# Second mixer: ScalarE takes eleven of VectorE's sixteen copies of the backward context columns

## The chip, the cores and the metric

The program runs on one core of a Trainium2 chip. The metric is the device time of one execution in microseconds; lower is better. A core has five engines with an instruction stream each: TensorE (PE in the profile, its weight loads PEld), VectorE (DVE), ScalarE (ACT), GpSimd (POOL) and SyncE (SP, which here only issues transfers). They meet through semaphores alone. TensorE writes its results to PSUM (eight banks of 512 fp32 columns on 128 partitions); VectorE and ScalarE read them from there.

## What is computed

The reference is a two-layer backbone over 512 latent and 256 context tokens of width 1024. Layer 0 is a recurrent and attention mixer with a mixture of experts (MoE) behind it; layer 1 is a grouped state-space mixer (S5) with a gated output (GLU) and a second MoE. The change lies in the S5 mixer. Cut to what matters:

```python
# 64 groups of 16 channels, 64 complex states each; once forward, once backward
for di, rev in enumerate((False, True)):
    _, h_ctx = s5_scan(u_c, lam_bar, b_bar, c_mat, h0, rev, False)   # context: 256 tokens
    yl_d, _  = s5_scan(u,   lam_bar, b_bar, c_mat, h_ctx, rev, True) # latents: 512 tokens
    y = y + yl_d
# s5_scan: h[t] = lam_bar * h[t-1] + b_bar @ u[t];  y[t] = Re(c_mat @ h[t])
glu(y)   # gelu, a 1024 x 2048 product, val * sigmoid(gate)
```

## The kernel before

The S5 mixer is the function `s5_mixer`. Tokens are taken in chunks of eight: the 256 context tokens make 32 chunks (NCC), the 512 latent tokens 64 (NCL), together 96 (NCK). For each of the 64 groups TensorE makes the state that a chunk adds to the recurrence. The forward direction lies on partitions 0 to 63 and the backward one on 64 to 127, so that both run in one scan over chunks. Real and imaginary part are two "parts" of a group.

Four groups make a half block (hb, sixteen of them, NHB), eight groups a block (b, eight of them, NB). The steps around the change, in order:

1. **Chunk sums.** For each hb TensorE waits for its factors in R (`r_in`, 512 KB a half block from HBM, seven buffers, a buffer loaded anew when the product that read it is done) and from hb 4 on for the copies of hb-4, since PSUM holds four half blocks. It then issues the products of lines 2478 and 2480 and raises `v_mm`.
2. **Copies out of PSUM into VH.** ScalarE makes two for each hb: line 2222, the latent columns of both directions (128 partitions, 512 elements), and line 2223, the forward context columns (64 partitions, 256 elements). Each raises `va_done`. VectorE makes the third, line 2350: the backward context columns (partitions 64 to 127, 256 elements), which raises `vd_done`. It waits for ScalarE's first copy of the same hb.
3. **Pairing** (`sweep`, lines 2337 to 2345). For each block b four VectorE operations (stages 0 to 3, 128 partitions, 752 elements) combine neighbouring chunks. Stage 0 waits for all copies of the block's two half blocks. VectorE's order is written out by hand: in the loop over hb each copy is followed, from hb 2 to 13, by a stage of blocks 0 to 3 (`divmod(hb - 2, 3)`, the fourth stage behind the third); blocks 4 to 7 follow when all copies are made.
4. **The scan** (lines 2374 to 2390) on VectorE: four levels over the context chunks, then 31 steps (STEPS) of four small operations in a chain.
5. **Filling in** (`fill`, lines 2400 to 2405, then `states`, line 2409) on VectorE, block by block, ScalarE making the other half of the states (line 2228). Ahead of it stands `dve.wait_ge(S['mod_mm'], LATE)`: the states are written to a tile, XS, in which weights of the modulation product have lain.
6. Meanwhile TensorE, when **all** copies of step 2 are made (`va_done`, `vd_done`), runs a chain of its own: for each block the product with the latents inside a chunk ("T", line 2506, a Toeplitz factor loaded by eight 64 KB transfers, line 2128), and between these the late modulation products n = 0 to 7 (LATE = 8; lines 1609 and 1613), for the parts of `mod_w` that the rest of layer 1 needs. Products 0 to 4 follow T(0) to T(4), one each; 5, 6 and 7 come together before T(5).
7. `from_states` (line 2520) adds the states' part for each block, `turn` (line 2531) transposes it after the gelu, and the GLU product (line 2551) starts when all eight blocks are turned.

SP's queue gives the order of transfers. Behind the R loads and the first two Toeplitz factors it waits for `v_mm` = 16, issues three 1 MB loads (line 2136), and then goes on as here:

```python
            for n in range(3, LATE):
                sp.wait_ge(S['mod_mm'], n - 2)
                sp.dma_start(w[n % 3], mod_weights(io, *MOD_LATE[n // 2], n % 2)).then_inc(m_in[n % 3], 16)
                toeplitz(n - 1)
            toeplitz(LATE - 1)
```

Each of these loads of modulation weights is 2 MB (line 2139), and `toeplitz(b)` waits for T(b-2). Products 0 to 2 read weights that ScalarE asked for before step 2 (line 2218).

Behind `turned` VectorE runs fifty small memsets (line 2425), each waiting for the one before, and only then waits for the first GLU product. The MoE behind the mixer is a loop over blocks of up to 64 or 128 tokens of one expert, six of each kind to a trip (UNROLL); its code is placed behind the mixer's in every engine's stream.

Of the kernel before, what the change touches and what calls it, by code (L numbers as in the profile page):

```python
# [10 lines left out]
ACT = mybir.ActivationFunctionType  # L11
AX = mybir.AxisListType

P = 128
# [2006 lines left out]
def s5_mixer(nc, io, st):  # L2021

    NCL, NCC = 64, 32
# [4 lines left out]
    with nc.cleanup_on_exit(), ctx:  # L2029
# [3 lines left out]
        def sem(name):  # L2033
            return nc.alloc_semaphore(f"{name}_s")
# [7 lines left out]
        VH = UV[:, NCK * SG:].rearrange("p (n a g) -> p n a g", a=2, g=SG)  # L2042
# [35 lines left out]
        S = {n: sem(n) for n in names.split()}  # L2078
# [7 lines left out]
        NHB, NB = SG // 4, SG // GB  # L2086
# [6 lines left out]

        LATE = 2 * len(MOD_LATE)

        def v_of(hb):
            return ps[:, (hb % 4) * 1024:(hb % 4 + 1) * 1024].rearrange("p (g a e) -> p g a e", g=4, a=2)

        def pairs(b):
            g = slice(b * GB, (b + 1) * GB)  # L2100
            return VH[:, 0:NCK - 2:2, :, g], VH[:, 1:NCK - 2:2, :, g]

        def scratch(j):
            return XS[:, j * NPAIR * 2 * GB:(j + 1) * NPAIR * 2 * GB].rearrange("p (n a g) -> p n a g", a=2, g=GB)

        def factor(level, which, n, g):
            return lam[:, level, which, :, g].rearrange("p (o a) g -> p o a g", o=1).to_broadcast([P, n, 2, GB])
# [70 lines left out]
        def _(act):  # L2178
# [40 lines left out]
            for hb in range(NHB):  # L2219
                act.wait_ge(S['v_mm'], hb + 1)  # L2220
                gs = slice(4 * hb, 4 * hb + 4)
                act.activation(VH[:, NCC:NCK, :, gs].rearrange("p c a g -> p g a c"), v_of(hb)[:, :, :, NCC:NCK], ACT.Copy).then_inc(S['va_done'], 1)
                act.activation(VH[0:64, 0:NCC, :, gs].rearrange("p c a g -> p g a c"), v_of(hb)[0:64, :, :, NCK:P], ACT.Copy).then_inc(S['va_done'], 1)

            def states(b):
                g = slice(b * GB, (b + 1) * GB)
                act.wait_ge(S['fill'], 4 * (b + 1))
                act.activation(SV[0:64, :, g, :], VH[0:64, NCC - 1:NCK - 1, :, g].rearrange("p c a g -> p a g c"),
                               ACT.Copy).then_inc(S['sf_done'], 1)
# [36 lines left out]
        def _(dve):  # L2266
# [60 lines left out]
            def sweep(b, stage):  # L2327
                even, odd = pairs(b)
                g = slice(b * GB, (b + 1) * GB)
                a, c = scratch(0), scratch(1)  # L2330
                n = 4 * (b - 0)
                if stage == 0:
                    if n:
                        dve.wait_ge(S['up'], n)
                    dve.wait_ge(S['va_done'], 4 * (b + 1))
                    dve.wait_ge(S['vd_done'], 2 * (b + 1))
                    dve.tensor_tensor(a, even, factor(0, 0, NPAIR, g), ALU.mult).then_inc(S['up'], 1)
                if stage == 1:
                    dve.tensor_tensor(c, even, factor(0, 1, NPAIR, g), ALU.mult).then_inc(S['up'], 1)
                if stage == 2:  # L2340
                    dve.wait_ge(S['up'], n + 1)
                    dve.tensor_tensor(a, a, odd, ALU.add).then_inc(S['up'], 1)
                if stage == 3:
                    dve.wait_ge(S['up'], n + 3)
                    dve.tensor_tensor(odd, a, c[:, :, ::-1, :], ALU.add).then_inc(S['up'], 1)

            dve.wait_ge(S['xres_in'], 16 * 8)
            for hb in range(NHB):
                dve.wait_ge(S['va_done'], 2 * hb + 1)
                dve.tensor_copy(VH[64:P, 0:NCC, :, 4 * hb:4 * hb + 4].rearrange("p c a g -> p g a c"), v_of(hb)[64:P, :, :, 0:NCC])\  # L2350
                   .then_inc(S['vd_done'], 1)
                if 2 <= hb < 14:
                    b, third = divmod(hb - 2, 3)
                    sweep(b, third)
                    if third == 2:
                        sweep(b, 3)
            for b in range(4, NB):
                for stage in range(4):
                    sweep(b, stage)
            dve.wait_ge(S['up'], 4 * NB)  # L2360
# [3 lines left out]
            for level in range(1, 5):  # L2364
# [3 lines left out]
                a, b = t1[:, 0:n], t2[:, 0:n]  # L2368
# [12 lines left out]
            for q in range(STEPS):  # L2381
                prev, here = VH[:, NCC - 1 + 2 * q], VH[:, NCC + 1 + 2 * q]
                a, b = t1[:, q % 2], t2[:, q % 2]
# [28 lines left out]
            def turned(b):  # L2412
                dve.wait_ge(S['zT_mm'], b + 1)
                dve.tensor_copy(zT[:, b, :], ps[:, b * 512:(b + 1) * 512]).then_inc(S['zt_dve'], 1)
# [6 lines left out]
            dve.wait_ge(S['o_mm'], NW)  # L2421
            for b in range(0, NB, 2):
                turned(b)
            for _ in range(50):
                done(dve.memset(sqr[:, 0, 0, 0:1], 0.0))
                done.wait()
            dve.wait_ge(S['gb_in'], 32)
            dve.wait_ge(S['xres_in'], 16 * 8)
            for u in range(8):
                n, m = divmod(u, 4)  # L2430
                val, gat = (ps[:, (2 * (u % 4) + j) * 512:(2 * (u % 4) + j + 1) * 512] for j in range(2))
                c = slice(n * 512, (n + 1) * 512)
                a, b = sv[u % 2], sg[u % 2]
# [14 lines left out]
        def _(pe):  # L2448
# [19 lines left out]
            for hb in range(NHB):  # L2468
                pe.wait_ge(S['u_done'], 16)
                pe.wait_ge(S['u_act'], 4)  # L2470
                pe.wait_ge(r_in[hb % NR], 16 * (hb // NR + 1))
                if hb >= 4:
                    pe.wait_ge(S['va_done'], 2 * (hb - 3))
                    pe.wait_ge(S['vd_done'], hb - 3)
                for g in range(4):
                    for part in range(2):
                        at = (hb % 4) * 1024 + g * 256 + part * P
                        pe.matmul(ps[0:64, at + NCC:at + P], Rb[hb % NR][:, g, part, 0:64], U[:, hb * 4 + g, :],
                                  start=True, stop=True, skip_group_check=True)
                        last = pe.matmul(ps[64:P, at:at + NCK], Rb[hb % NR][:, g, part, 64:P], U[:, hb * 4 + g, ::-1],  # L2480
                                         start=True, stop=True, skip_group_check=True)
                last.then_inc(S['v_mm'], 1)
            pe.wait_ge(S['va_done'], 2 * NHB)
            pe.wait_ge(S['vd_done'], NHB)

            def out_of(b, h, q):
                return ps[64 * h:64 * h + 64, b * 512 + q * P:b * 512 + (q + 1) * P]
# [70 lines left out]
def program(nc, io, out):  # L2558
# [4 lines left out]
    with ExitStack() as ctx:  # L2563
        x = ctx.enter_context(nc.sbuf_tensor("x", [P, NT0, D], F32))
        cT = ctx.enter_context(nc.sbuf_tensor("cT", [P, KD, 2], F32))
        io['modrow'] = dram('modrow', (2, 2, 6 * D))
        io['s5_r'] = dram('s5_r', (P, SG // 4, 4 * 2 * P))
        io['s5_w'] = dram('s5_w', (P, SG // GB, 2 * SL * GB * SI))
        io['s5_kt'] = dram('s5_kt', (SG, 32, 15 * SI))
        io['s5_l8'] = dram('s5_l8', (P, 4 * SG))  # L2570
        moe_h, table = dram('moe_h', (NTOK, D)), dram('item_table', (P, 8), I32)
        moe_acc = [dram(f'moe_acc{k}', (NTOK, D)) for k in range(2)]
        io['primer'] = dram('primer', (4, P))

        def x_final(t):

            steps = out[0].rearrange("(c s) d -> s c d", s=SL)
            return [(slice(64 * j, 64 * j + 64), steps[2 * t + j]) for j in range(2)]

        with ExitStack() as early:  # L2580
            head = {name: early.enter_context(nc.sbuf_tensor(name, shape, F32)) for name, shape in
                    (('rows', [P, NT0, D]), ('ident', [P, P]), ('modc', [P, 2, 2, KD]))}
            prepare(nc, io, {'x': x, 'cT': cT, **head})
            mixer0(nc, io, {'x': x, **head})
        moe_blocks(nc, io, {'x': x, 'moe_h': moe_h, 'moe_acc': moe_acc, 'item_table': table},
                   0, NTOK, NT0 - NL)
        s5_mixer(nc, io, {'x': x, 'cT': cT, 'moe_acc': moe_acc})
        moe_blocks(nc, io, {'x': x, 'moe_h': moe_h[0:LAT], 'moe_acc': [a[0:LAT] for a in moe_acc], 'item_table': table,
                            'x_out': x_final}, 1, LAT, 0)
# [15 lines left out]
```

## Time and profile before

| | |
|---|---|
| median of 3 runs | 2506.55 us (2506.09 to 2510.54) |
| the profiled execution | 2506.16 us, its span 2504.4 us |
| mean granted clock of TensorE | 0.952 |
| TensorE, VectorE, ScalarE, GpSimd busy | 86%, 44%, 20%, 17% of the span |
| the stretch of the chunk sums and their copies | 1515.9 to 1548.8 us |
| pairing / scan / filling in | to 1563.4 / 1606.3 / 1638.6 us |
| GLU product | from 1645.5 us |

Times within the execution count from the start of the span. In a row "idle before" is the time that the engine stood still ahead of an instruction, with the one that ended it. A granted clock of 1.00 is 2.4 GHz, 0.50 is 1.2 GHz.

### The profile page before, as it was taken

Reading aid. Unit: us, or ns where it says so; the run is one execution under the profiler, and the core shown is the slowest. Engines: PE = TensorE matmul, PEld = TensorE weight load, DVE = VectorE, ACT = ScalarE, POOL = GpSimd, SP = SyncE. Lnnn points to the kernel's source line nnn. Section 1 sums busy time; section 2 is a strip of 40 time slices with the busy share of each in tenths; the row PEclk is TensorE's granted clock in tenths of the full one; section 3 lists DMA queues with packets and bytes.
Section 4 is the critical chain, followed back from the end, with each engine's and each line's share of the span. In section 5 each row is a group of like instructions: output and inputs, shape, how many; then the busy total and the mean of one; then the engine's idle time right before and its main releaser. Section 6 shows DMA issues by size and latency. Waiting matters only on the chain. (4 is left out here: it accounts for less than half of the span.)

```text
span 2504.4 us, 40476 instructions
## 1 busy us (share of the span) xinstructions
PE 2143.6 (86%) x11989; PEld 1189.9 (48%) x11990; DVE 1092.3 (44%) x2311; ACT 509.8 (20%) x945; POOL 433.9 (17%) x359
## 2 busy tenths in 40 slices
PE   5889999997999999999999816699789999988874
PEld 3765444744544444444444405354444444444442
DVE  8853365944543333333333338942532222222222
ACT  3443233611121111111111125220221111100000
POOL 1000000002012222222222210000122222232332
PEclk9999999998999999999999968799799999999997
DMA  9971002003799999999999669830499999899996
GB/s 358 386 265 46 34 34 84 1 1 131 264 346 355 354 358 357 359 351 350 355 358 358 202 158 329 275 146 0 160 404 375 361 363 358 274 390 372 385 385 207
DMA packets 173622, 666.72 MB, mean 266 GB/s; under 512 B 37666, under 2 KB 48898, under 8 KB 129882
## 3 DMA queue, kind: packets, MB, share of 16 engines
q1 hardware_dynamic: 121410, 564.71, 58.7%
q0 software_dynamic: 36160, 64.84, 11.0%
q10 hardware_dynamic: 15960, 35.96, 4.1%
q8 instruction: 56, 0.92, 0.1%
q14 instruction: 36, 0.29, 0.0%
HBM read 617.29 MB, written 86.09 MB: 281 GB/s over the span
## 5 line engine op out<-in xcount | busy, mean ns | idle before, releaser
L1518 PE MATMUL banks_l<-slotw_l,xTw_l 128*128 128x512 f32 x800 | 358.2, 601 | 27.7 <-issue 27.7
L1529 PE MATMUL banks_l<-slotn_l,xTn_l 128*64 128x256 f32 x2816 | 325.0, 383 | 34.5 <-issue 34.5
L1529 PEld LDWEIGHTS banks_l<-slotn_l,xTn_l 128*64 128x64 f32 x2816 | 212.0, 137 | 178.9 <-issue 104.8
L1518 PEld LDWEIGHTS banks_l<-slotw_l,xTw_l 128*128 128x128 f32 x800 | 148.5, 191 | 239.3 <-issue 239.3
L1568 PE MATMUL banks_l<-slotn_l,late_l 128*64 128x512 f32 x704 | 189.9, 615 | 19.6 <-DVE late_l L1356 17.9
L1547 PE MATMUL banks_l<-slotw_l,late_l 128*128 128x512 f32 x400 | 191.8, 602 | 15.4 <-DVE late_l L1338 15.4
L977 POOL DMA_INDIRECT xgw_l<-moe_h,idxw_l x58 | 60.6, 1045 | 741.0 <-PE banks_l L1463 367.1
L1005 POOL DMA_INDIRECT moe_acc<-late_l,idxn_l x88 | 151.2, 1718 | 190.5 <-DMA moe_acc<-late_l,idxn_l 172.5
L937 POOL IOTA slotw_l<- 128x1 f32 x2 | 0.3, 140 | 729.1 <-POOLq L69 431.3
L1335 DVE TENSOR_TENSOR late_l<-late_l,banks_l 128x256 f32<-128x256 f32 x50 | 21.0, 421 | 240.2 <-ACT late_l L1107 240.2
L556 PE MATMUL ps_a<-W_a,hT_a 128*128 128x512 f32 x288 | 124.9, 595 | 0.0
L1107 ACT ACTIVATE late_l<-banks_l 128x256 f32<-128x256 f32 x50 | 19.2, 384 | 509.6 <-PE banks_l L1518 509.6
L983 POOL DMA_INDIRECT xgn_l<-moe_h,idxn_l x96 | 103.4, 1077 | 83.5 <-DVE idxn_l L1285 56.1
L1270 DVE TENSOR_TENSOR onehotn_l<-iota_slot_l,rank_l 128x512 bf16 (+1 forms) x98 | 79.3, 809 | 86.2 <-issue 86.2
L2551 PE MATMUL ps_s<-UV_s,ZU_s 128*128 128x512 f32 x256 | 110.1, 592 | 0.7 <-ACT ZU_s L2238 0.7
L1112 ACT ACTIVATE late_l<-banks_l 128x128 f32<-128x128 f32 x88 | 24.4, 278 | 417.5 <-PE banks_l L1529 417.5
L1547 PEld LDWEIGHTS banks_l<-slotw_l,late_l 128*128 128x128 f32 x400 | 68.5, 191 | 71.3 <-issue 71.3
L994 POOL DMA_INDIRECT moe_acc<-yw_l,idxw_l x50 | 79.4, 1589 | 131.3 <-DVE yw_l L1362 131.3
L1045 ACT ACTIVATE xTw_l<-banks_l 128x512 f32<-128x512 f32 x108 | 64.5, 598 | 153.1 <-PE banks_l L1463 148.6
L1338 DVE COPY late_l<-banks_l 128x256 f32<-128x256 f32 x50 | 21.2, 425 | 160.2 <-PE banks_l L1537 160.2
L1263 DVE TENSOR_TENSOR onehotw_l<-iota_slot_l,rank_l 128x768 bf16 (+1 forms) x60 | 51.9, 865 | 84.4 <-issue 84.4
L556 PEld LDWEIGHTS ps_a<-W_a,hT_a 128*128 128x128 f32 x288 | 55.3, 192 | 68.4 <-issue 68.0
(433 smaller groups left out, 3235.0 us busy)
## 6 DMA issues: line engine op xcount, KB each, us to landing
slotn_l<-in_exp_w_gate SPq DMA_DIRECT2D x88, 1024.0 KB
slotn_l<-in_exp_w_up SPq DMA_DIRECT2D x88, 1024.0 KB
slotn_l<-in_exp_w_down SPq DMA_DIRECT2D x88, 1024.0 KB, 12.1
slotw_l<-in_exp_w_gate SPq DMA_DIRECT2D x50, 1024.0 KB
slotw_l<-in_exp_w_up SPq DMA_DIRECT2D x50, 1024.0 KB
slotw_l<-in_exp_w_down SPq DMA_DIRECT2D x50, 1024.0 KB
w_p<-in_mod_w SPq DMA_DIRECT2D x12, 2048.0 KB, 15.4
W_a<-in_ar_w_in SPq DMA_DIRECT2D x5, 2048.0 KB, 9.4
```

The lines of the kernel that those rows point to most:

```text
L556: last = pe.matmul(bank(n % 4), hT[:, k, t * P:(t + 1) * P], W[:, c % 2, k, :], start=(k == 0), stop=(k == KD - 1))
L977: pool.indirect_dma_start(xg_w[b % 3][:], None, h_dram, bass.IndirectOffsetOnAxis(idx[0][b][:].bitcast(U32), 0), bounds_check=last_row, oo ...
L983: pool.indirect_dma_start(xg_n[b % 3][:], None, h_half, bass.IndirectOffsetOnAxis(idx[1][b][:].bitcast(U32), 0), bounds_check=last_half, o ...
L994: pool.indirect_dma_start(accs[0], bass.IndirectOffsetOnAxis(idx[0][b][:].bitcast(U32), 0), y_w[b % 2][:], None, bounds_check=last_row, oo ...
L1005: pool.indirect_dma_start(acc_half, bass.IndirectOffsetOnAxis(idx[1][b][:].bitcast(U32), 0), y_n[b % 2], None, bounds_check=last_half, oob ...
L1045: act.activation(xT_w[b % 2][:, 4 * half:4 * half + 4, :], pT_w.rearrange("p (k c) -> p k c", c=P), ACT.Copy).then_inc(W['xT_done'], 1)
L1270: dve.tensor_tensor(onehot[1][:].rearrange("p t (a s) -> p t a s", a=2), where, rank[:, :, bass.ds(e, 1)].rearrange("p t (a o) -> p t a o" ...
L1518: last = pe.matmul(pGU_w, xT_w[b % 2][:, k, :], wgu[0][b % WIDE_RING][:, :, k, :], start=(k == 0), stop=(k == KD - 1))
L1529: last = pe.matmul(pGU_n[H * side:H * side + H, b % 2], xT_n[b % 2][:, k % 4, H * (k // 4):H * (k // 4) + H], w[:, :, k, P * side:P * side ...
L1547: last = pe.matmul(pY_w[:, half * 512:(half + 1) * 512], hidT_w[:, k, :], wd[0][b % WIDE_RING][:, k, half * 512:(half + 1) * 512], start=( ...
L1568: last = pe.matmul(pY_n[H * side:H * side + H, :], hidT_n[:, H * k:H * k + H], w[:, k, side * 512:(side + 1) * 512], start=(k == 0), stop= ...
L2551: last = pe.matmul(ps[:, (2 * (u % 4) + half) * 512:(2 * (u % 4) + half + 1) * 512], zT[:, k, m * P:(m + 1) * P], glu[n][:, k, half, :], s ...
```

## The change

ScalarE makes the copy of the backward context columns for the eleven half blocks that are not in `DVE_CTX`; VectorE keeps it for 2, 5, 8, 11 and 14. The waits on `va_done` and `vd_done` are counted accordingly. VectorE's order becomes one block after the other: the copies that are left to it of the block's two half blocks, then the block's four stages. The number of memsets behind `turned` goes from 50 to 56. No transfer is added, removed or moved.

```diff
+        DVE_CTX = (2, 5, 8, 11, 14)
+
+        def ctx_copied(hb):
+            return sum(k <= hb for k in DVE_CTX)
+
+        def evicted(hb):
+            return 3 * (hb + 1) - ctx_copied(hb)
...
                 act.activation(VH[0:64, 0:NCC, :, gs].rearrange("p c a g -> p g a c"), v_of(hb)[0:64, :, :, NCK:P], ACT.Copy).then_inc(S['va_done'], 1)
+                if hb not in DVE_CTX:
+                    act.activation(VH[64:P, 0:NCC, :, gs].rearrange("p c a g -> p g a c"), v_of(hb)[64:P, :, :, 0:NCC], ACT.Copy)\
+                       .then_inc(S['va_done'], 1)
...
-                    dve.wait_ge(S['va_done'], 4 * (b + 1))
-                    dve.wait_ge(S['vd_done'], 2 * (b + 1))
+                    dve.wait_ge(S['va_done'], evicted(2 * b + 1))
+                    if ctx_copied(2 * b + 1):
+                        dve.wait_ge(S['vd_done'], ctx_copied(2 * b + 1))
...
-            for hb in range(NHB):
-                dve.wait_ge(S['va_done'], 2 * hb + 1)
-                dve.tensor_copy(VH[64:P, 0:NCC, :, 4 * hb:4 * hb + 4].rearrange("p c a g -> p g a c"), v_of(hb)[64:P, :, :, 0:NCC])\
-                   .then_inc(S['vd_done'], 1)
-                if 2 <= hb < 14:
-                    b, third = divmod(hb - 2, 3)
-                    sweep(b, third)
-                    if third == 2:
-                        sweep(b, 3)
-            for b in range(4, NB):
+            for b in range(NB):
+                for hb in (2 * b, 2 * b + 1):
+                    if hb in DVE_CTX:
+                        dve.wait_ge(S['va_done'], evicted(hb - 1) + 1)
+                        dve.tensor_copy(VH[64:P, 0:NCC, :, 4 * hb:4 * hb + 4].rearrange("p c a g -> p g a c"), v_of(hb)[64:P, :, :, 0:NCC])\
+                           .then_inc(S['vd_done'], 1)
                 for stage in range(4):
                     sweep(b, stage)
...
-            for _ in range(50):
+            for _ in range(56):
...
-                    pe.wait_ge(S['va_done'], 2 * (hb - 3))
-                    pe.wait_ge(S['vd_done'], hb - 3)
+                    pe.wait_ge(S['va_done'], evicted(hb - 4))
+                    if ctx_copied(hb - 4):
+                        pe.wait_ge(S['vd_done'], ctx_copied(hb - 4))
...
-            pe.wait_ge(S['va_done'], 2 * NHB)
-            pe.wait_ge(S['vd_done'], NHB)
+            pe.wait_ge(S['va_done'], evicted(NHB - 1))
+            pe.wait_ge(S['vd_done'], ctx_copied(NHB - 1))
```

## Rows read from the trace of the kernel before

**Rows 1.** The page: busy time of the engines, share of the span, instructions.

```profile
PE 2143.6 (86%) x11989; PEld 1189.9 (48%) x11990; DVE 1092.3 (44%) x2311; ACT 509.8 (20%) x945; POOL 433.9 (17%) x359
```

**Rows 2.** Groups of instructions, 1400 to 1700 us: busy us, mean ns | idle before.

```profile
L2350 DVE COPY UV_s<-ps_s 64x256 f32<-64x256 f32 x16 | 9.7, 605 | 7.7 <-ACT UV_s L2222 7.3
```

**Rows 3.** VectorE in order of time: start, us, what, idle before.

```profile
1523.89 0.62 DVE L2350 COPY UV_s<-ps_s 64x256 f32<-64x256 f32 x1 [0.80 <-ACT UV_s L2222]
1524.54 0.94 DVE L2337 TENSOR_TENSOR XS_s<-UV_s,lam_s 128x752 f32<-128x752 f32 x1
...
1529.73 0.61 DVE L2350 COPY UV_s<-ps_s 64x256 f32<-64x256 f32 x1
...
1548.85 0.94 DVE L2337 TENSOR_TENSOR XS_s<-UV_s,lam_s 128x752 f32<-128x752 f32 x1
...
1552.50 0.94 DVE L2337 TENSOR_TENSOR XS_s<-UV_s,lam_s 128x752 f32<-128x752 f32 x1
...
1606.36 0.69 DVE L2400 TENSOR_TENSOR Rall_s<-UV_s,lam_s 128x512 f32<-128x512 f32 x1
...
1637.24 1.35 DVE L2409 COPY XS_s<-UV_s 64x1024 f32<-64x1024 f32 x1
...
1644.59 6.21 DVE L2425 MEMSET sqr_s<- 128x1 f32 x50
1659.67 0.69 DVE L2435 TENSOR_TENSOR Rall_s<-ps_s,x 128x512 f32<-128x512 f32 x1 [8.87 <-PE ps_s L2551]
```

**Rows 4.** ScalarE in order of time.

```profile
1521.37 1.08 ACT L2222 ACTIVATE UV_s<-ps_s 128x512 f32<-128x512 f32 x1 [1.06 <-PE ps_s L2480]
...
1524.11 1.11 ACT L2222 ACTIVATE UV_s<-ps_s 128x512 f32<-128x512 f32 x1
1525.02 0.66 ACT L2223 ACTIVATE UV_s<-ps_s 64x256 f32<-64x256 f32 x1
1525.48 1.15 ACT L2222 ACTIVATE UV_s<-ps_s 128x512 f32<-128x512 f32 x1
...
1547.18 1.02 ACT L2222 ACTIVATE UV_s<-ps_s 128x512 f32<-128x512 f32 x1
```

**Rows 5.** TensorE in order of time.

```profile
1532.55 0.27 PE L2478 MATMUL ps_s<-UV_s,Rall_s 128*64 128x96 f32 x1 [1.33 <-DVE UV_s L2350]
...
1548.92 1.09 PE L2506 MATMUL ps_s<-Tb_s,UV_s 128*64 128x128 f32 x16 [1.78 <-DVE UV_s L2350]
...
1567.66 1.97 PE L2506 MATMUL ps_s<-Tb_s,UV_s 128*64 128x128 f32 x16 [12.51 <-DMA Tb_s<-s_kt]
...
1584.91 1.33 PE L2506 MATMUL ps_s<-Tb_s,UV_s 128*64 128x128 f32 x10 [4.58 <-DMA Tb_s<-s_kt]
...
1600.15 3.45 PE L1613 MATMUL ps_s<-ZU_s,cT 128*2 128x256 f32 x32 [5.73 <-DMA ZU_s<-in_mod_w]
```

**Rows 6.** SyncE's issues in order of time (start, time over which it issued, count).

```profile
1552.35 0.39 SPq L2139 DMA_DIRECT2D ZU_s<-in_mod_w  x1
...
1573.44 0.39 SPq L2139 DMA_DIRECT2D XS_s<-in_mod_w  x1
...
1590.61 0.39 SPq L2139 DMA_DIRECT2D ZU_s<-in_mod_w  x1
```

**Rows 7.** Stretches: busy us and counts by engine, PEclk, DMA share, GB/s.

```profile
1549.00:1555.20 6.20, 6.15 (x104) 3.31 (x104) 6.10 (x8) 0.00 (x0) 0.00 (x0) 1.00 0.98 373
1555.20:1567.60 12.40, 0.00 (x0) 0.00 (x0) 12.08 (x13) 1.50 (x4) 0.00 (x0) 0.65 1.05 329
...
1968.00:2088.00 120.00, 114.55 (x521) 56.62 (x522) 31.70 (x83) 14.49 (x30) 31.61 (x24) 1.00 0.98 360
```

**Rows 8.** The Toeplitz loads of line 2128 (64 of them): issue to landing.

```profile
DMA to landing us min/median/max: 2.2/7.7/11.7
```

**Rows 9.** Instruction fetches by the DMA queues: whole span (page), then 1968 to 2504 us.

```profile
q8 instruction: 56, 0.92, 0.1%
...
q8 instruction: 1, 0.02, 0.0%
```

## The prediction, made before the changed kernel ran

> **What bounds the kernel now.** The page comes first: TensorE is busy for 86% of the span, VectorE for 44% [rows 1]. These are averages over stages, so the stage of the change has to be read by itself. The chain of waits that the page gives reaches back only to about 1760 us, behind the mixer; for the mixer I follow the waits by hand, through the orders of time of the engines and of SP's queue.
>
> Between 1515.9 and 1548.8 us three engines share the work. VectorE's sixteen copies have a mean of 605 ns [rows 2], and one of ScalarE of the same size reads 0.66 us [rows 4]. What counts is the step from one start to the next: on ScalarE 0.91 us after line 2222 and 0.46 after line 2223 (1524.11, 1525.02, 1525.48) [rows 4], on VectorE 0.65 us after line 2350 (1523.89 to 1524.54) [rows 3]. VectorE has no gap here, since the stages of pairing stand between its copies; it is the late engine here, and it ends the pairing at 1563.45 (1548.85 plus the four blocks left at 3.65 us each) and the scan at 1606.36, where the first fill starts [rows 3].
>
> TensorE is late for another reason. The row at 1532.55 names VectorE's copy as the releaser [rows 5], but the copy it needs (hb 5) had ended at 1530.34 [rows 3]; what it waits for besides is the R load of hb 9, so that one came last. From hb 9 on R loads set TensorE's pace, and the change doesn't touch them. Two things decide the rest:
>
> - The first fill needs the end of VectorE's scan (1606.36) **and** the eighth late modulation product, which starts at 1600.15 and ends at 1603.60 [rows 5]. The second is only 2.75 us earlier. A shorter VectorE chain can't bring more than these 2.75 us.
> - The modulation products hang on T(0), which starts at 1548.92, released by VectorE's **last copy** [rows 5]. From there the chain is: product 0 done, SP issues load 3 at 1552.35, behind it the eight loads of T(2); T(2) at 1567.66; product 2 done, load 5 issued at 1573.44 with T(4)'s behind it; T(4) at 1584.91, product 4 done, load 7 issued at 1590.61, product 7 at 1600.15 [rows 5, 6].
>
> From the fills to the GLU product VectorE sets the pace again: from 1606.36 to the last `states` at 1637.24 it runs seven blocks and the four fill operations of the eighth (4 x 0.69), 4.0 us a block [rows 3], with ScalarE and TensorE waiting for it in each block. What the first fill gains or loses, the GLU product at 1645.5 and all behind it gain or lose.
>
> **The change, part by part.**
>
> *VectorE's chain.* Eleven copies go, 11 x 0.65 = 7.15 us. The first stage can start when ScalarE has made hb 1's third copy: hb 1 starts on ScalarE at 1521.37 [rows 4], and 0.91 + 0.46 + 0.66 later at about 1523.4, stage 0 of block 0 starts, where it now starts at 1524.54. From there: eight blocks of 3.65 us (1548.85 to 1552.50) [rows 3] and five copies of 0.65 make 29.2 + 3.25, so pairing ends at 1555.85 instead of 1563.45, 7.6 us earlier, if VectorE never waits.
>
> *ScalarE.* Eleven copies more. The trace has no ScalarE copy of partitions 64 to 127; the nearest row is line 2223, of the same form on the other half: 0.46 us a step, at most the full 0.66 [rows 4]. A half block takes 1.83 us (0.91 + 0.46 + 0.46) with three copies and 1.37 with two. From hb 1 at 1521.37 ScalarE then works without a gap to hb 7: five times 1.83 and two times 1.37 make 11.9, so hb 7 is done at 1533.5 with the tail of its last copy, and hb 3 at 1526.6. VectorE wants them for block 3 at 1535.7 and for block 1 at 1527.8. Later ScalarE follows the R loads as now; hb 15 starts at 1547.18 [rows 4] and is done at 1549.2, wanted at 1552.2. VectorE doesn't wait; at 0.66 a step (0.2 more for each of eleven) blocks 1 and 3 would still be in time. ScalarE's added 5.1 us lie beside VectorE's work.
>
> *TensorE in the chunk sums.* VectorE's copy of hb 2 now stands behind the whole of block 0: it ends at 1527.7, so hb 6 starts at 1527.8 instead of 1526.5, and hb 7 and 8 about 1.2 and 0.8 us late. The copy of hb 5 ends at 1532.1, just before the R load of hb 9; hb 12 waits 0.5 us for the copy of hb 8 (1540.0). SP issues R loads of 13 to 15 up to 1.4 us later, but behind others still queued at a DMA share of 1.0. I cost all of this at nothing, as the R loads hide it; uncovered it would be 1.3 us.
>
> *The last copy.* This is the wait that the block order adds. VectorE's copy of hb 14 comes behind the stages of block 6: 1523.4 + 7 x 3.65 + 5 x 0.65 = 1552.2. All TensorE's work from T(0) on waits for it, and behind TensorE stand load 3 and T(2)'s loads on SP's queue. T(0) moves from 1548.92 to 1552.3, **3.4 us late**. In that time TensorE is idle from 1547.1 on, 5.2 us. Now it works at a granted clock of 1.00 from 1549.0 to 1555.2; in the 12.4 idle us behind that the mean was 0.65, which is 3.7 us at 1.00 and 8.7 at 0.50 [rows 7]. So I take T(0) and product 0 at 0.50, as T(2) and product 2 now run: 1567.66 to 1573.4, 5.7 us, instead of 1548.92 to 1552.3, 3.4 us [rows 5, 6]. Load 3 is then issued at 1558.0 instead of 1552.35, 5.7 us late.
>
> *What reaches the first fill.* The 5.7 us are an upper bound. Now load 3 is queued behind three 1 MB loads while the DMA share is 0.98, and T(2) comes 15.3 us after it is issued (1552.35 to 1567.66). For load 5, with less ahead of it, the time to T(4) is 11.5 us (1573.44 to 1584.91). With 11.5 us, T(2) comes at 1569.5, **1.9 us late**. The lower bound is 0, if what is in the queue sets T(2)'s time alone. I take 1.9, since the row of load 5 is the nearest to a shortened queue. From T(2) on each link is a wait for a landing and moves along, so product 7 ends at 1605.5 and the first fill starts at 1605.6 instead of 1606.36.
>
> *Memsets.* Six more at 6.21 / 50 = 0.12 us make 0.75 us. They are hidden in the 8.87 us in which VectorE waits for the first GLU product [rows 3]; with that cover gone they would cost 0.75 us.
>
> *Place of the code.* ScalarE's stream gets eleven instructions, VectorE's loses eleven copies and gets six memsets with their waits, TensorE's loses two waits; the MoE's loops move by that much. In the trace instructions are fetched 56 times by q8 over the span and once after 1968 us, while the loops run several trips [rows 9]: a trip fetches nothing now. Hence 0. The Trainium skill ("Runtime: NRT & Kernel Launch", "Instruction fetch mechanics") says that a taken branch whose target lies outside the two 16 KiB pages held makes the engine wait for a fetch. By that rule a moved loop could begin to fetch in each trip; the trace shows no such fetch before, and what a move does no row shows.
>
> **Sum.** 1606.36 - 1605.6 = 0.75 us gained at the first fill, nothing added or lost behind it: 2506.16 - 0.75 = 2505.4 us for the profiled execution. That one lay 0.4 us below the median, so I give **2505.8 us**.
>
> **Rivals.**
>
> - *No slip.* The queue hides the late T(0) wholly; the first fill starts at 1603.65, gain 2.7 us: 2503.8 us. For it: the DMA share of 0.98 to 1.05 up to T(2) [rows 7]. Against it: the queued 3 MB last only some 8 us at 373 GB/s, to about 1557, before load 3 would be issued.
> - *Full slip.* Every link comes 5.7 us late; the first fill starts at 1609.3, 3.0 us later than now: 2509.5 us. For it: each link is a wait. Against it: load 3 no longer queues.
> - *The whole 7.6 us arrive.* 2499.0 us. It needs the modulation chain 5 us earlier as well, and nothing makes it so.
> - *A moved loop fetches code, the other side.* Place: the MoE's loops. The smallest landing among the Toeplitz loads is 2.2 us [rows 8]; in the three trips with wide blocks, in which TensorE is busy for 114.55 of 120 us [rows 7], little covers a stall. One fetch a trip: 3 x 2.2 = 6.6 us, 2512.4 us with the gain taken off. It decides from 5 us, 1.7 us a trip. For it: all three streams change length. Against it: no fetch in a trip now. The skill's rule above is the same mechanism; it names no time for it.
>
> **Chances.** Forecast 0.42, no slip 0.18, full slip 0.19, the whole gain or one like it 0.08, moved loop 0.13. A difference of 0.2%, 5.0 us, is about what a measurement of this kernel can tell from none. The first three lie within it: same 0.79, faster 0.08, slower 0.13. Range: the three give 2503.8 to 2509.5; with 1.5 us to each side for the spread of the runs and to meet the other two partly, 2502.0 to 2511.0.
>
> **What the profile after would show.** Line 2350 five times, a third ScalarE copy eleven times at 0.65 us; the last stage of pairing ending at about 1555.9 and the scan at 1598.8; T(0) at 1552.3 at half clock; load 3 at 1558, T(2) at 1569.5; product 7 ending at 1605.5 and the first fill right behind it with VectorE idle for some 7 us. VectorE idle within pairing would say that ScalarE or TensorE is the bound there. The prediction is wrong if the first fill moves by more than 3 us either way, or if the GLU product moves as said and the end doesn't, which would put the cause in the MoE.

## The result and the profile after

The kernel after takes 2551.62 us (median of 4 runs, 2549.41 to 2556.01), the kernel before 2506.32 us (4 runs, 2501.57 to 2510.54). The ratio is 1.0177, with an interval of 1.0153 to 1.0201: slower by 45 us, far outside the range on record. The profiled execution of after has a span of 2547.7 us, 43.3 more than before.

**Where the 45 us are.** I measure marks from the start of the first chunk sum (1515.9 us before, 1516.7 after). The first fill comes 90.5 us behind it before and 90.7 after; the GLU product 129.6 and 132.0; the last wide block of the second MoE 642.7 and 648.6; the last narrow block 958.4 and **1002.7**; the end 988.5 and 1031.0. So the mixer gives away 2.4 us, and the narrow blocks of the second MoE 38 us, in a loop that the diff doesn't touch.

The page of after has one line that is out of proportion. First the page of before, its count of 8 KB instruction fetches (packets, MB, share), which stands beside that of [rows 9]:

```profile
q14 instruction: 36, 0.29, 0.0%
```

The page of after, its span, the busy line that answers to [rows 1], and both kinds of instruction fetch:

```profile
span 2547.7 us, 40481 instructions
...
PE 2151.4 (84%) x11989; PEld 1190.5 (47%) x11990; DVE 1084.5 (43%) x2306; ACT 516.3 (20%) x956; POOL 437.5 (17%) x359
...
q8 instruction: 56, 0.92, 0.1%
...
q14 instruction: 78, 0.64, 0.1%
```

The engines do the same work, and one fetch queue has 42 packets more. The view of VectorE's waits in the second MoE says who pays (idle us, times, longest one). Before:

```profile
DVE late_l L1346 <- issue: 3.0, 1, 3.0
```

After:

```profile
DVE late_l L1346 <- issue: 58.5, 7, 10.3
...
DVE late_l L1335 <- issue: 21.2, 2, 10.8
```

"issue" is time in which the engine waited for nothing that the profile shows. VectorE's order of time in after shows where in a trip it lies:

```profile
1986.52 0.42 DVE L1335 TENSOR_TENSOR late_l<-late_l,banks_l 128x256 f32<-128x256 f32 x1 [10.44 <-issue]
...
2108.97 0.42 DVE L1335 TENSOR_TENSOR late_l<-late_l,banks_l 128x256 f32<-128x256 f32 x1 [10.75 <-issue]
...
2197.25 0.69 DVE L1270 TENSOR_TENSOR onehotn_l<-iota_slot_l,rank_l 128x512 bf16 x1 [0.85 <-issue]
2208.02 0.29 DVE L1346 TENSOR_TENSOR late_l<-late_l,banks_l 128x128 f32<-128x128 f32 x1 [10.08 <-issue]
...
2217.99 0.29 DVE L1346 TENSOR_TENSOR late_l<-late_l,banks_l 128x128 f32<-128x128 f32 x1 [1.95 <-ACT late_l L1112]
...
2268.96 0.29 DVE L1346 TENSOR_TENSOR late_l<-late_l,banks_l 128x128 f32<-128x128 f32 x1 [10.21 <-issue]
...
2329.48 0.29 DVE L1346 TENSOR_TENSOR late_l<-late_l,banks_l 128x128 f32<-128x128 f32 x1 [10.30 <-issue]
```

A trip of the loop makes several blocks, and the wait stands once in a trip, at the first VectorE instruction that the trace shows behind the jump back; the same line in the next block (2217.99) waits for ScalarE as it always did. Eight trips begin behind a jump; seven of them wait 9.96 to 10.75 us, the last 5.94. Eight times five packets are 40 of the 42 new ones.

What the wait does to the rest is in the windows of 2200 to 2300 us (busy us of PE, PEld, DVE, ACT, POOL, then TensorE's clock, DMA share, GB/s). Before:

```profile
2200.00:2300.00 100.00, 80.50 (x546) 46.71 (x542) 27.12 (x78) 9.62 (x22) 29.64 (x22) 0.98 1.00 379
```

After:

```profile
2200.00:2300.00 100.00, 71.16 (x462) 38.80 (x458) 23.66 (x69) 8.74 (x20) 26.05 (x20) 0.91 0.88 326
```

Before, the DMA engines are busy without a gap, and as I read it they set the pace there; after, they stand still for 12% of the time. The last part of the result is the mixer, in VectorE's order of time, to be laid beside [rows 3]:

```profile
1524.14 0.94 DVE L2349 TENSOR_TENSOR XS_s<-UV_s,lam_s 128x752 f32<-128x752 f32 x1 [7.54 <-ACT UV_s L2233]
...
1552.65 0.59 DVE L2364 COPY UV_s<-ps_s 64x256 f32<-64x256 f32 x1
...
1607.38 0.69 DVE L2408 TENSOR_TENSOR Rall_s<-UV_s,lam_s 128x512 f32<-128x512 f32 x1 [7.49 <-PE ps_s L1613]
```

TensorE's, beside [rows 5]: T(0), T(2), T(7), `from_states(5)` and the GLU product:

```profile
1553.34 1.97 PE L2515 MATMUL ps_s<-Tb_s,UV_s 128*64 128x128 f32 x16 [4.94 <-DVE UV_s L2364]
...
1571.34 1.98 PE L2515 MATMUL ps_s<-Tb_s,UV_s 128*64 128x128 f32 x16 [9.06 <-DMA Tb_s<-s_kt]
...
1615.73 1.97 PE L2515 MATMUL ps_s<-Tb_s,UV_s 128*64 128x128 f32 x16 [4.84 <-DMA Tb_s<-s_kt]
...
1636.46 2.71 PE L2529 MATMUL ps_s<-Wb_s,XS_s 128*64 128x128 f32 x32 [2.60 <-DMA Wb_s<-s_w]
...
1648.65 3.70 PE L2560 MATMUL ps_s<-UV_s,ZU_s 128*128 128x512 f32 x8 [0.70 <-ACT ZU_s L2249]
```

And SP's issues, beside [rows 6]: load 3, then the GLU weights and behind them the last three factors.

```profile
1559.49 0.39 SPq L2147 DMA_DIRECT2D ZU_s<-in_mod_w  x1
...
1617.75 1.01 SPq L2158 DMA_DIRECT2D UV_s<-in_s_glu_w  x2
...
1620.90 4.55 SPq L2165 DMA_DIRECT2D Wb_s<-s_w  x2
```

Pairing starts and ends early as said, T(0) comes late as said, the first fill hardly moves. New against this trace of before is the wait of 2.60 us of `from_states(5)` for its factor. In TensorE's order of time in before the same product starts without one, behind `turn(3)`:

```profile
1631.68 1.15 PE L2531 MATMUL ps_s<-ident_s,ZU_s 64*64 64x64 f32 x32 [1.00 <-ACT ZU_s L2233]
1632.95 1.97 PE L2520 MATMUL ps_s<-Wb_s,XS_s 128*64 128x128 f32 x32
```

One trace of before is not enough to call the 2.4 us at the GLU product an effect of the change. Among the nine traces with the old order of the mixer (this one and eight of the experiments) the GLU product comes between 128.8 and 134.8 us behind the first chunk sum, and five of them show a wait of that product for its factor, 0.16 to 2.82 us long.

### The profile page after: what moved, and what is told of

It is laid out like the page before. It is cut to its first block and busy times, and to the rows that moved or that the text cites. A ratio compares the mean times of both kernels' runs of the same rounds, so it can differ in the third digit from the quotient of the medians.

```text
span 2547.7 us, 40481 instructions
## 1 busy us (share of the span) xinstructions
PE 2151.4 (84%) x11989; PEld 1190.5 (47%) x11990; DVE 1084.5 (43%) x2306; ACT 516.3 (20%) x956; POOL 437.5 (17%) x359
## 5 line engine op out<-in xcount | busy, mean ns | idle before, releaser
L1568 PE MATMUL banks_l<-slotn_l,late_l 128*64 128x512 f32 x704 | 198.6, 641 | 19.8 <-DVE late_l L1356 17.8
L1005 POOL DMA_INDIRECT moe_acc<-late_l,idxn_l x88 | 157.4, 1789 | 64.9 <-DMA moe_acc<-late_l,idxn_l 39.0
L1049 ACT ACTIVATE xTn_l<-banks_l 128x512 f32<-128x512 f32 x92 | 54.9, 597 | 177.7 <-PE banks_l L1469 176.0
```

The costliest lines, as they stand in the source:

```text
L1005: pool.indirect_dma_start(acc_half, bass.IndirectOffsetOnAxis(idx[1][b][:].bitcast(U32), 0), y_n[b % 2], None, bounds_check=last_half, oob ...
L1568: last = pe.matmul(pY_n[H * side:H * side + H, :], hidT_n[:, H * k:H * k + H], w[:, k, side * 512:(side + 1) * 512], start=(k == 0), stop= ...
```

## The experiments

**The theory after the result.** The change takes eleven copies and one wait out of VectorE's stream, and adds six memsets: 2253 instructions become 2247, and VectorE's loop of the second MoE (351 instructions) begins at its instruction 1887, not 1893. (These are counts of the program as it is handed to the compiler; experiment 4 comes to the compiled code.) There it fetches code in every trip. Rivals: ScalarE's loop, which moves from 961 to 972, does it; or the new order in the mixer leaves something behind that slows the MoE.

**1. After, with the loop back at 1893.** The memsets of line 2432 are the handle: one more moves the loop by one.

```
-            for _ in range(56):
+            for _ in range(62):
```

> The changed kernel with 62 memsets instead of 56, nothing else. This puts VectorE's loop of the second MoE back at the place in its instruction stream that it has in the kernel before (instruction 1893 instead of 1887); ScalarE's loop stays 11 instructions further on. Theory A (VectorE's moved loop fetches its code anew in each trip): no VectorE wait of about 10 us at the start of a trip, instruction fetches by q14 back from 78 to about 36, time 2505 to 2508 us. Rival B (ScalarE's loop, moved by 11, is what costs): nothing changes, about 2551 us, q14 about 78. Rival C (the mixer's new order leaves the MoE in a worse state, by its loads or clock): about 2551 us as well, but the first fill is where it is in the changed kernel in any case (about 1607).

Measured: 2512.99 us (10 runs, 2507.31 to 2516.91) against 2505.95 (19 runs) of before, ratio 1.003 (1.0017 to 1.0043). The page of this run says

```profile
q14 instruction: 37, 0.30, 0.0%
```

Six memsets more give 39 of the 45 us back. The fetches go and the waits with them, while the mixer's new order stays.

**2. Before, with the loop at 1887.** The kernel before, with nothing of the change:

```
-            for _ in range(50):
+            for _ in range(44):
```

> The kernel before with 44 memsets instead of 50, nothing else: VectorE's second MoE loop begins at instruction 1887, as in the changed kernel; no copy is moved. Theory A: about 2551 us, nine VectorE waits of about 10 us, q14 fetches about 78. Rivals B and C: 2506 us, since neither ScalarE's stream nor the mixer's order is touched.

Measured: 2548.34 us (4 runs), ratio 1.0189 (1.0157 to 1.0221). Its page, and its view of waits:

```profile
q14 instruction: 79, 0.64, 0.1%
```

```profile
DVE late_l L1346 <- issue: 56.2, 6, 10.3
...
DVE late_l L1335 <- issue: 20.4, 2, 10.2
```

Six memsets fewer make the kernel before as slow as the one after, in the same places: eight waits, not the nine that I had expected, since the first trip doesn't begin behind a jump back. The place alone does it.

**3. Before, with ScalarE's loop at 972.**

```
+            for k in range(11):
+                act.wait_ge(S['warm'], k + 1)
+                act.activation(warm[:], ident[0:1, 0:1], ACT.Copy).then_inc(S['warm'], 1)
```

> The kernel before with eleven one-element ScalarE copies behind the last sigmoid of the mixer, each waiting for the one before: ScalarE's second MoE loop begins 11 instructions later, as in the changed kernel; VectorE's stays. They cost at most about 11 x 0.25 = 3 us if nothing hides them. Theory A: 2506 to 2509 us, q14 about 36. Rival B: about 2551 us with the fetches. Rival C: as A.

Measured: 2508.84 us (10 runs), ratio 1.001 (0.9998 to 1.0022), 36 packets of 8 KB as before. ScalarE's move is not the cause.

**4. Which places fetch.** The kernel before with other numbers of memsets (`range(47)`, `range(70)`, `range(24)`, `range(82)`, `range(192)`, `range(222)`), one run of each:

> The kernel before with 47 memsets: VectorE's loop begins at instruction 1890, half way between the place without fetches (1893) and the one with (1887). Theory A says that the loop either keeps its code or fetches in each trip, with nothing between: either about 2506 us with 36 fetches by q14 or about 2548 with 78, which of them places the edge. Rival (a cost that grows with the distance moved): about 2527 us.

> The kernel before with 70 memsets: VectorE's loop begins at 1913, 20 instructions later. Theory A with an edge just under 1893: still without fetches, about 2506 us (20 memsets more take 2.5 us of the 8.87 us wait). Rival (only the tuned place is good, any other costs): about 2548 us.

> The kernel before with 24 memsets: VectorE's loop begins at 1867, 20 instructions under the place that fetched (1887). If the stretch of bad places is broad (the loop of 351 instructions lies across one page of 128 more): fetches in each trip, about 2545 us, q14 about 78. If it is a narrow one: about 2506 us, q14 about 36.

> The kernel before with 82 memsets: VectorE's loop begins at 1925, 12 instructions behind the last place known to be good (1913) and 35 to 38 behind the edge. A loop of 351 instructions keeps within three pages of 128 at 34 places in a row only, so if crossing into a fourth page is what makes it fetch, this one fetches again: about 2548 us, q14 about 78. If the start of the loop alone decides: about 2506 to 2510 us, q14 about 36.

> The kernel before with 192 memsets in place of 50, so that the loop of VectorE in the second MoE begins at its instruction 2035 (before: 1893) and ends 350 later. Question: where do the places with a fetch in every trip begin again? Theory A, two aligned pages of 256 instructions: the step between 1887 and 1890 is the start of a page (about 1888), the next pages start at about 2144 and 2400; a loop of 351 lies within two pages when it begins between 1888 and 2400 - 351 = 2049, so 2035 fetches nothing: about 37 packets on the queue of 8 KB instruction fetches, no waits of 10 us at the first VectorE instruction of a trip. Theory B, no such pages, the good places are a strip that ends somewhere above 1925: 78 or so packets and nine waits of some 10 us. By both the memsets themselves cost 142 x 0.124 = 17.6 us less the idle 8.9 us of before, some 9 us: by A about 2515 us, by B about 2560 us.

> The same with 222 memsets: the loop begins at 2065, 177 or so behind the step near 1888. Theory A (two aligned pages of 256 instructions from 1888 on): 2065 + 351 = 2416 lies beyond 2400, three pages are touched, so the loop fetches in every trip: about 78 packets on the queue of 8 KB fetches and nine waits of some 10 us, 2515 + 4 + 43 = about 2562 us. Theory B (only where the start lies against some other mark counts, not where the loop ends): no fetches, about 2519 us, or fetches in both this and the run with 192 memsets.

| loop begins at | in the compiled code | packets of 8 KB | time, us |
|---|---|---|---|
| 1867 | 1833 | 79 | 2547.83 |
| 1887 | 1853 | 79 | 2548.34 (4 runs) |
| 1890 | 1856 | 37 | 2505.06 |
| 1893 (before) | 1859 | 36 | 2506.32 (4 runs) |
| 1913 | 1879 | 37 | 2509.58 |
| 1925 | 1891 | 36 | 2504.71 |
| 2035 | 2001 | 37 | 2513.34 |
| 2065 | 2031 | 37 | 2503.72 |

A side result: the 222 memsets of the last row take 27.74 us, where 50 took 6.21 [rows 3], and the one run of it shows no loss. In its trace the GLU product still takes 109.5 us, as in before, so the cover there is deeper than the 8.87 us that I had counted on. The run with 192 memsets is slower, but in its trace the GLU product already starts 5.2 us late, ahead of the memsets.

The run at 1867 shows what the 10 us are made of. VectorE's order of time, the start of one trip:

```profile
2205.14 0.29 DVE L1346 TENSOR_TENSOR late_l<-late_l,banks_l 128x128 f32<-128x128 f32 x1 [5.47 <-issue]
2209.99 0.29 DVE L1356 COPY late_l<-banks_l 128x128 f32<-128x128 f32 x1 [4.56 <-issue]
...
2218.37 0.29 DVE L1346 TENSOR_TENSOR late_l<-late_l,banks_l 128x128 f32<-128x128 f32 x1 [1.63 <-ACT late_l L1112]
```

Twenty places earlier the wait splits into 5.5 and 4.6 us at two instructions, and one packet of 8 KB moves in each of these waits (windows of 2 us from 2202 and from 2206). In after, the single wait of 10.08 us that ends at 2208.02 likewise holds two packets (windows from 2200 and from 2206). So a trip pays for two fetches one after the other, some 5 us each; the other three of its five packets fall where nobody waits. The page's start at 1855 explains the split, as I read it. In the run at 1867 the first instruction shown (line 1346) is number 1842 of the compiled code and the second (line 1356) number 1863, so each waits for a page of its own; in after the loop begins at 1853, two instructions ahead of that page's start, and both pages are needed before anything that the trace shows.

**5. The mixer: the last copy on ScalarE.** In run 1 the change is 7 us slower than before with the fetches gone. Is it the last copy, behind the stages of block 6? (62 memsets in place of 56 are in this and the next two, one more here, so that the loop begins at 1893.)

```
-        DVE_CTX = (2, 5, 8, 11, 14)
+        DVE_CTX = (2, 5, 8, 11)
```

> The changed kernel with VectorE's loop of the second MoE at its old place (1893) and with hb 14's copy given to ScalarE too: DVE_CTX = (2, 5, 8, 11), 63 memsets. Theory A for the rest of the loss (T(0) waits for VectorE's copy of hb 14, and what TensorE asks for behind it comes late: in the run with 62 memsets T(0) came 36.7 us after the first chunk sum instead of 33.0, the GLU product 133.0 instead of 129.6): T(0) at +33 to 34, the first fill at +87.5 to 88.5 instead of +90.5, right behind the eighth modulation product, the GLU product at +127 to 128, the time 2 to 3 us under the kernel before and 5 to 6 under the run with 62 memsets. Rival (ScalarE's third copies slow the mixer, or GLU loads and not T(0) are late): the GLU product stays at about +132 to 133 and the time at about 2510.

Measured: 2512.72 us (12 runs) against 2506.4 (23), ratio 1.0017 (1.0001 to 1.0033). T(0) comes 34.6 us behind the first chunk sum (said: 33 to 34), the first fill 88.7, 1.8 earlier than before, and the GLU product at 131.4, 1.8 later, where 127 to 128 was said. The gain at the fill is lost before the GLU product: `from_states(5)` waits 4.07 us for its factor in this trace.

**6. The mixer: VectorE's copies one block earlier.**

```
-                for hb in (2 * b, 2 * b + 1):
+                for hb in (2 * b + 2, 2 * b + 3):
```

> The changed kernel with 62 memsets and VectorE's five copies each made one block earlier in its order (hb 14 ahead of block 6's stages instead of behind them); the share of the copies is unchanged. Theory A (the order puts the last copy behind the pairing, not the share): T(0) at +33 to 34, first fill at +87.5 to 88.5, GLU product at +127 to 128, time as in the run without hb 14 among VectorE's. Rival (the share itself, eleven ScalarE copies, costs): GLU product at about +132.

Measured: 2509.26 us (12 runs), ratio 1.0007 (0.9991 to 1.0023). The first fill comes at 86.7 us, 3.8 earlier than before; the GLU product at 129.3, only 0.3 earlier (said: 127 to 128). So the expected gain failed here too, and the rival's 132 didn't come either. TensorE's order of time in this run, T(0), the eighth modulation product, `from_states(5)`, the GLU product:

```profile
1551.24 1.92 PE L2515 MATMUL ps_s<-Tb_s,UV_s 128*64 128x128 f32 x16 [3.66 <-DVE UV_s L2364]
...
1599.50 3.38 PE L1613 MATMUL ps_s<-ZU_s,cT 128*2 128x256 f32 x32 [5.61 <-DMA ZU_s<-in_mod_w]
...
1633.35 3.57 PE L2529 MATMUL ps_s<-Wb_s,XS_s 128*64 128x128 f32 x32 [3.85 <-DMA Wb_s<-s_w]
...
1645.59 9.71 PE L2560 MATMUL ps_s<-UV_s,ZU_s 128*128 128x512 f32 x22 [0.70 <-ACT ZU_s L2249]
```

and SP's issues:

```profile
1613.35 1.01 SPq L2158 DMA_DIRECT2D UV_s<-in_s_glu_w  x2
...
1616.57 4.73 SPq L2165 DMA_DIRECT2D Wb_s<-s_w  x2
```

The fills run ahead, and `from_states(5)` waits 3.85 us for a factor of 1 MB queued behind 4 MB of GLU weights. Those are issued only when all of `T` is done.

**7. The same, with the factor of block 5 ahead of the GLU weights.**

```
-            sp.wait_ge(S['t_mm'], NB)
-            sp.wait_ge(S['rec'], CTX_OPS + 1)
-            glu_half(0)
             for b in range(NW, NB):
                 sp.wait_ge(S['o_mm'], b - NW + 1)
                 sp.dma_start(Wb[b % NW], ...)
+                if b == NW:
+                    sp.wait_ge(S['t_mm'], NB)
+                    sp.wait_ge(S['rec'], CTX_OPS + 1)
+                    glu_half(0)
```

> The run with the copies a block ahead, with one more change in SP's order: the first GLU half (two 2 MB loads) is issued behind the load of from_states(5)'s factor, not ahead of it. In the run without this the first fill came at +86.7 us, 3.8 earlier than in the kernel before, but the GLU product at +129.3, only 0.3 earlier, since TensorE waited 3.85 us for that factor. Theory (the loads queued behind 4 MB of GLU weights hold from_states(5)): no such wait, GLU product at +125.5 to 126.5, behind the last fill as in the kernel before (39.1 us from the first fill), time about 3 to 4 us under the kernel before. Rival (TensorE's own order of from_states and turns is the bound, or the GLU weights then come late): GLU product at +128 or later.

Measured: 2508.47 us (11 runs), ratio 1.0011 (1.0002 to 1.002). SP's issues, and TensorE's `from_states(6)`:

```profile
1622.05 0.32 SPq L2162 DMA_DIRECT2D Wb_s<-s_w  x1
1622.48 1.91 SPq L2158 DMA_DIRECT2D UV_s<-in_s_glu_w  x2
1624.43 6.60 SPq L2162 DMA_DIRECT2D Wb_s<-s_w  x1
```

```profile
1643.11 3.68 PE L2530 MATMUL ps_s<-Wb_s,XS_s 128*64 128x128 f32 x32 [4.24 <-DMA Wb_s<-s_w]
```

The wait has moved from block 5 to block 6, whose factor now stands behind the same 4 MB. The GLU product comes at 134.2 us, 4.6 later than before, where 125.5 to 126.5 was said; the first fill is at 89.5 in this trace, which the edit doesn't explain. That TensorE waits for a factor queued behind the GLU weights is shown; that the GLU product can be had earlier is not. No version beats the kernel before: the medians of the four lie 1.8 to 7.0 us above it, and three of the four intervals lie above 1.

## Why the prediction was wrong

**What held.** Stage 0 of pairing 7.4 us behind the first chunk sum (1524.14; said: 1523.4, which is 7.5 behind it in before), no wait of VectorE within pairing, so ScalarE is no bound. T(0) 3.6 us late behind the last copy (said 3.4) and at the slow clock: 1.97 us where it took 1.09 [rows 5]. Load 3 at 1559.49, measured from the first chunk sum 6.3 us late (said 5.7). From there to T(2) 11.85 us (taken: 11.5, from load 5 [rows 6]), so T(2) 2.9 us late (said 1.9). First fill 0.2 us later than before (said 0.75 earlier), with VectorE idle for 7.49 us ahead of it (said: some 7). The clock shows in the windows of after, T(0) and the stretch ahead of it:

```profile
1553.00:1555.30 2.30, 1.96 (x20) 1.66 (x24) 2.17 (x4) 0.00 (x0) 0.00 (x0) 0.50 1.01 427
1549.00:1553.30 4.30, 0.00 (x0) 0.00 (x0) 4.17 (x5) 1.53 (x3) 0.00 (x0) 0.87 0.91 346
```

The second row has no TensorE work at all; the first has the granted clock at 0.50, the lower level of 1.2 GHz.

**The step that failed: "a trip fetches nothing now. Hence 0."** The first half is true of the kernel before and says nothing of a loop that has moved. I read only the queue of 16 KB fetches [rows 9], on which nothing changed and whose 56 packets are as many as TensorE's own compiled code fills; the loop's fetches go by the other queue, with 8 KB packets. Runs 1 and 2 show the cause from both sides: six memsets in or out, and nothing else, switch 39 and 42 us. The sign, mechanism and place were in the rival of the moved loop, at a chance of 0.13 and 6.6 us. Its size was wrong three times over:

- one fetch of 2.2 us a trip was really two in a row, some 5 us each. The 2.2 us were the smallest landing of a row whose median is 7.7 [rows 8], and the loop's fetches go beside transfers that keep the DMA engines busy (share 1.03 in the window of one wait below);
- three trips with wide blocks became eight of the nine trips;
- I put the cost where TensorE is busiest. The two waits in wide trips cost 3.4 us together (last wide block at 648.6 less start at 335.5, against 642.7 less 333.0). The narrow blocks cost 38 us.

Why it is so, one wait of each kind in after shows. In a wide trip TensorE has products left that don't hang on VectorE, and waits 1.64 us of the 10.44. In the window of the narrow trip's wait it is busy for 2.42 of 10 us (the first number behind the 10.00):

```profile
1987.00 0.50 PE L1537 MATMUL banks_l<-ident_l,late_l 128*128 128x128 f32 x2 [1.64 <-DVE late_l L1335]
```

```profile
2198.00:2208.00 10.00, 2.42 (x24) 1.57 (x19) 0.00 (x0) 0.28 (x1) 1.59 (x1) 0.81 1.03 398
```

The DMA engines are busy through that wait (1.03) and have gaps behind it (0.88 over the 100 us above). Without the waits their share is 1.00 in the narrow trips, so what isn't moved there isn't made up later.

The eight waits sum to 77.7 us; 45 reach the end. Part of the rest was waited before as well (2.41 us for ScalarE at line 1346 in most narrow blocks of before, 5.7 at line 1335 in the wide ones), and, as I read it, what is loaded ahead carries TensorE part of the way.

The rule of the Trainium skill that the prediction cites ("Runtime: NRT & Kernel Launch", "Instruction fetch mechanics": a taken branch to a target outside the two pages held forces a fetch) has its mechanism confirmed here, by runs 1 and 2. Taken as aligned pages of 256 instructions its 16 KiB pages fit all eight places of experiment 4. The packets that carry VectorE's loop don't fit them: they have 8 KB, and five move in a trip, so here the measurement says 8 KB.

**The second step that failed, a small one:** "What the first fill gains or loses, the GLU product … gain or lose." Between them stands a second chain, T(7), GLU weights, the factors of blocks 5 to 7. It hangs on T(0) and not on the fill, and after the change it is last: T(7) is late, the weights and the factors are issued late (1617.75 and 1620.90), and TensorE waits 2.60 us. In the trace of before that wait doesn't exist, so I didn't see the chain. It is near even with the old order: in the two of the nine old-order traces in which T(0) came latest (34.2 and 35.0 us behind the first chunk sum, 33.0 in before) TensorE waits 2.82 and 2.49 us for the same factor and the GLU product comes at 133.1 and 134.8. With the new order all five traces show a wait for a factor, 2.60 to 4.24 us. So the chain is shown, but what it costs the changed kernel, 2.4 us in this trace, lies within the spread of traces with the old order. In run 5 all that was gained at the fill (1.8 us) was gone at the GLU product, in run 6 nearly all (3.5 of 3.8 us).

**What stays open.** Run 1 is 7 us over before (4 to 11 by the interval), of which its trace places 3.4 at the GLU product; where the rest lies I can't say, since the profiled execution of that run was its fastest. Run 5 shows no more at the GLU product than 1.8 and has a ratio of 1.0017. Between executions the stretch from the GLU product to the shared expert's first product alone takes 140.1 to 145.6 us, whatever the mixer's order. The difference lies in the transposes and router products at its end: the granted clock there was 0.59 in before (145.4 us) and 0.86 in the run with 222 memsets (140.1 us). That hides differences of this size in one trace. Which rule sets the edge of the places that fetch stays open too.

## What to carry to other kernels

An edit ahead of a runtime loop changes where the loop lies in each engine's instruction stream, and a loop of some hundred instructions can then fetch its code in every trip: count each engine's instructions before and after (for a rule about pages, in the compiled code and not in the program), compare the instruction-fetch packets of both pages, and look for "issue" waits that stand once in a trip. Where they differ, pad the stream with a few cheap instructions before judging the edit itself; here that is the difference between 1.8% and 0.3%. And before a gain at one join is carried to the end, look for every other chain that meets it later, also those that wait for nothing now.

## What the runs showed of the hardware

- Three instructions decide between 37 and 79 packets of 8 KB and between 2505 (one run) and 2548 us (loop at 1890 or 1887), in a kernel that is otherwise the same.
- A fetch of 8 KB of code beside DMA engines with a share of 1.03 holds VectorE for some 5 us (5.47 and 4.56 us in the run at 1867, 10.08 for two in after); the packets themselves are nothing (0.64 MB in all, 0.1% of the engines' time).
- Fetches come in packets of 8 KB on one queue and of 16 KB on the other (q14 and q8 of the pages); only the first changed with the place of VectorE's loop.
- A loop of 399 instructions of the same engine, earlier in the same stream, makes its trips without such fetches, and one of 351 doesn't: length alone doesn't decide.
